# Differential attention in a two-block fp32 kernel: first branch weighed behind the bias pass, adaptive rows one by one, another order at the heads' ends and in the merge

## The chip, the cores and the metric

One core of a Trainium2 chip runs the whole program. The metric is the device time of one execution in microseconds (us); the figure given for a kernel is the median of its runs.

## The reference, cut to what matters

Two transformer blocks over 1024 tokens of width 1024, all in fp32. The change lies in the first block's mixer, whose three branches are merged under sigmoid gates:

```
h = rmsnorm(x); z = h @ w_in; gates = sigmoid(h @ w_gate + b_gate)     # 3 x 1024 gate columns
y_a = gmlp_mixer(...)                 # 256 wide
y_b = pool_mixer(...)                 # 256 wide
y_c = diff_attn_mixer(...)            # 4 heads, two softmaxes each: a = p0 - lam * p1, out = a @ v, rmsnorm
merged = g_a * (y_a @ proj_a) + g_b * (y_b @ proj_b) + g_c * (y_c @ proj_c)
x = x + merged @ w_out
```

The second block needs `ada_params(silu(c), w_ada, b_ada)` and the same for a context vector: products of a vector of 1024 with matrices of 1024 x 3072, which depend on nothing of the first block. The kernel computes them early, beside the first block's attention.

## The kernel before, in words

Every engine has a program of its own, written out by hand, and they meet only at semaphores. There is no scheduler: what stands first in an engine's program runs first.

**Dense units.** A unit is 1024 x 128 weights (512 KB). SyncE (SP) loads it, GpSimd (POOL) splits it into a high and a low part (lines 505 and 507), TensorE (PE) multiplies with three passes, 24 matmuls of 512 columns for each half of the tokens (line 530). The split of a unit begins when PE opens the unit before it. Results go to the PSUM halves 0 and 1. A half may be overwritten when its reader has counted `dn_out[half]`; `dense_order()` writes the order of the units down, and `dense` waits for the turn before it in the same half.

**The attention phase ("diff").** Four heads, each with eight tiles `t` of 128 queries; tile `t` has (t+1)*128 keys. In a tile the engines do:

- PE (`diff_head` of the tensor block): `turn_weights` transposes the weights of tile t (line 691; it waits for `aa_ready` and for PSUM pair 1, that is for the copy of the last product), a dense block in slot 0, `weigh_values` (line 700), the scores of tile t+2 (line 666), a dense block in slot 1.
- VectorE (DVE): `biased(h, t+1)` adds the bias to the scores and takes the row maxima (line 1740, twice), negates them (line 1744, 128x2); `combine(h, t+1)` follows ScalarE's exponentials (lines 1753 to 1756) and counts `aa_ready`; then the copy of the product (line 1800), then in slot 0 and slot 1 what the dense blocks need of VectorE.
- ScalarE (ACT): the copy of the transposed weights (line 1245), `exps(h, t+1)` (line 1228), the tanh of the gate blocks (line 1163).

**What fills the slots.** `head_slots()` deals out the blocks of each index i: gates `ga`, `gb`, `gc` (24 matmuls a half, read by ScalarE), and `pa`, `pb`, the projections of the first and the second branch (one unit together, 6 matmuls a half, so 12 in a slot). VectorE weighs `pa` and `pb` with their gates (`weighted`, line 1765) and adds them (line 1770). So `pb` in slot 1 needs `pa` weighed, and the next tile's gate block needs `pb` weighed. In this text a tile with `pa` in one slot and `pb` in the other is a pair tile; there are two of them in each head (tiles 2 and 6, in the last head 3 and 6).

**The adaptive rows.** 48 tiles of 128x1024 (`AW`, two buffers), loaded by SP with `load_ada`, reduced by `ada` on VectorE against the vector CL, and where k % 6 < 2 against CC too (line 1783: one pass or two). They run in pairs, one pair in each of the first 24 tiles, behind the copy of the product. The load of row k waits until row k-2 is done; it stands in SP's queue behind the tile's weight loads.

**Heads' ends and starts.** Behind tile 7 VectorE makes the norm's diagonal (line 1604), waits for PE's spread (line 571), and scales and splits the head's output (lines 1813, 1818). `head_start` then makes the values and the first scores, transposes the values (line 683), and ScalarE copies them to VC (line 1236) and frees the PSUM pair (line 1238), before the first `turn_weights`.

**The merge.** For each i of eight, VectorE takes `pc` of half 0 and half 1 times its gate (line 1859), adds it to M (line 1865), and then makes the low part of the M before (`merged_low`, line 1870), which waits for ScalarE's high part.

The slots, the places of the rows and the merge's loop are set by these lines of the kernel before:

```
        for place in [(t, 1) for t in range(2)][:len(free) - len(blocks)]:
            free.remove(place)
        for i in range(KC):
            merge(i)
            if i:
                merged_low(i - 1)
```

Of the kernel before, what the change touches and what calls it, by code (L numbers as in the profile page):

```python
# [27 lines left out]
P = 128  # L28
# [84 lines left out]
ADA_STEP = 2  # L113
# [3 lines left out]
def head_slots():  # L117
# [9 lines left out]
    for h in range(HEADS_C):  # L127
# [9 lines left out]
        for place in [(t, 1) for t in range(2)][:len(free) - len(blocks)]:  # L137
            free.remove(place)
# [5 lines left out]
SLOTS = head_slots()  # L144

# [43 lines left out]
def build(nc, t_in, out):  # L189
# [219 lines left out]
    def _(sp):  # L409
# [44 lines left out]
        step = 0  # L454
        for h in range(HEADS_C):
            for t in range(QT_N):
# [3 lines left out]
                if step == 0:  # L460
# [50 lines left out]
    def _(pe):  # L511
# [159 lines left out]
        def head_start(h):  # L671
# [32 lines left out]
        def diff_head(h):  # L704
            for t in range(QT_N):
                turn_weights(h, t)
                slot(h, t, 0)
# [5 lines left out]
                slot(h, t, 1)  # L713
# [368 lines left out]
    def _(act):  # L1082
# [91 lines left out]
        for j in range(2):  # L1174
            xts[0] += 1
            act.wait_ge(xt, xts[0])
            act.activation(YA[:, j * T:(j + 1) * T], TMP[j], ACT.Copy).then_inc(hi, 1)

# [61 lines left out]
        def diff_head(h):  # L1240
            last = h == HEADS_C - 1
            for t in range(QT_N):
                n = (t + 1) * P
                act.wait_ge(done[1], before("diff", 1) + 17 * h + 2 + 2 * t)
# [7 lines left out]
                slot(h, t, 0)  # L1252
# [30 lines left out]
        for half in range(2):  # L1283
            gate_out("ga", 0, half)
# [262 lines left out]
    def _(v):  # L1547
# [229 lines left out]
        def ada(k):  # L1777
# [14 lines left out]

        def diff_head(h):
            for t in range(QT_N):
                if t + 1 < QT_N:
                    v.wait_ge(done[1], before("diff", 1) + 17 * h + 2 + 2 * t)
                    biased(h, t + 1)
                    combine(h, t + 1)
# [4 lines left out]
                slot(h, t, 0)  # L1803
                step = h * QT_N + t
# [625 lines left out]
```

## Time and profile before

| | |
|---|---|
| median of 3 runs | 2733.97 us (2733.26 to 2734.22) |
| profiled execution | 2733.36 us, its span 2731.5 us |
| busy: PE, VectorE, ScalarE, GpSimd | 2564.0, 1375.3, 696.0, 660.6 us |
| granted TensorE clock, mean of the span | 0.978 |
| bytes moved | 158.16 MB, mean 58 GB/s |

The span is the profiled execution from its first to its last instruction; the time is the whole of that execution. PE is busy for nearly all of the span, so what counts is the time in which PE stands still, and the stretches in which its clock is granted at half (0.50, which is 1.2 GHz, where 1.00 is 2.4 GHz). The attention phase and the merge lie between 137 and 800 us of the span. A timeline row gives start, duration, engine, line, operation and count, and in brackets how long the engine had been idle before it and for whom.

### The profile page before, as it was taken

Reading aid. Unit: us, or ns where it says so; the run is one execution under the profiler, and the core shown is the slowest. Engines: PE = TensorE matmul, PEld = TensorE weight load, DVE = VectorE, ACT = ScalarE, POOL = GpSimd, SP = SyncE. Lnnn points to the kernel's source line nnn. Section 1 sums busy time; section 2 is a strip of 40 time slices with the busy share of each in tenths; the row PEclk is TensorE's granted clock in tenths of the full one; section 3 lists DMA queues with packets and bytes.
Section 4 is the critical chain, followed back from the end, with each engine's and each line's share of the span. In section 5 each row is a group of like instructions: output and inputs, shape, how many; then the busy total and the mean of one; then the engine's idle time right before and its main releaser. Section 6 shows DMA issues by size and latency. Waiting matters only on the chain.

```text
span 2731.5 us, 32633 instructions
## 1 busy us (share of the span) xinstructions
PE 2564.0 (94%) x12342; PEld 2106.0 (77%) x12342; DVE 1375.3 (50%) x1730; ACT 696.0 (25%) x973; POOL 660.6 (24%) x368
## 2 busy tenths in 40 slices
PE   7989998999899999999999989989999998899997
PEld 4867777777778788888888867878888887688876
DVE  5646363644364453145315564256676664533344
ACT  3222222222212111000000132145556652222121
POOL 1322222222233233333333332200000002222221
PEclk9999999999999999999999999999999999999998
DMA  4134242421322111111121111100000001110111
GB/s 154 47 101 139 85 124 93 131 93 47 133 68 85 46 46 46 54 46 46 48 67 46 54 56 33 45 24 9 8 15 8 8 9 56 31 39 31 38 39 69
DMA packets 44734, 158.16 MB, mean 58 GB/s; under 512 B 5453, under 2 KB 6733, under 8 KB 44527
## 3 DMA queue, kind: packets, MB, share of 16 engines
q1 hardware_dynamic: 38172, 132.94, 15.7%
q10 hardware_dynamic: 6482, 24.12, 2.4%
q8 instruction: 55, 0.90, 0.1%
q14 instruction: 25, 0.20, 0.0%
HBM read 143.67 MB, written 13.37 MB: 57 GB/s over the span
## 4 chain that ended last, share of the span: by engine, by line
PE 85%; DVE 9%; issue 3%; ACT 2%; DVEq 0%; ACTq 0%
PE PS L530 65%; PE PS L965 4%; PE PS L905 3%; PE PS L937 2%; PE PS L913 2%; PE PS L666 1%; PE PS L571 1%; PE PS L700 1%; PE PS L563 1%; DVE H L1626 1%; DVE SC L1783 1%; PE PS L691 1%; DVE PT L2118 1%; PE PS L1047 1%; PE PS L1062 0%
## 5 line engine op out<-in xcount | busy, mean ns | idle before, releaser
L530 PE MATMUL PS<-H,w_hl 128*128 128x512 f32 x6624 | 1548.9, 394 | 41.8 <-DVE H L1626 16.7
L530 PEld LDWEIGHTS PS<-H,w_hl 128*128 128x128 f32 x6624 | 1245.3, 189 | 327.8 <-issue 43.2
L505 POOL CAST w_hl<-w_raw 128x1024 fp32r<-128x1024 f32 x180 | 199.0, 1106 | 1997.2 <-PE PS L530 1587.0
L507 POOL TENSOR_TENSOR w_hl<-w_raw,w_hl 128x1024 fp32r<-128x1024 f32 x180 | 452.5, 2514 | 14.4
L530 PE MATMUL PS<-FF,w_hl 128*128 128x512 f32 x1056 | 239.8, 389 | 0.0
L530 PEld LDWEIGHTS PS<-FF,w_hl 128*128 128x128 f32 x1056 | 198.3, 188 | 41.1
L905 PE MATMUL PS<-CKV,QN 128*128 128x512 f32 (+1 forms) x576 | 146.9, 369 | 4.4 <-DVE QN L2082 4.4
L1360 ACT ACTIVATE SC<-SC,vec 128x1024 f32<-128x1024 f32 x22 | 25.4, 1153 | 392.5 <-DVE SC L1975 392.4
L965 PE MATMUL PS<-PT,CKT 128*128 128x256 f32 x960 | 121.4, 284 | 4.1 <-DVE PT L2118 4.1
L965 PEld LDWEIGHTS PS<-PT,CKT 128*128 128x128 f32 x960 | 117.7, 191 | 8.0 <-DVE PT L2118 7.3
L2118 DVE TENSOR_TENSOR PT<-PS,PT 128x512 fp32r<-128x512 f32 (+1 forms) x192 | 103.6, 595 | 30.6 <-ACT PT L1454 30.0
L905 PEld LDWEIGHTS PS<-CKV,QN 128*128 128x128 f32 x576 | 101.5, 193 | 22.2 <-issue 4.8
L2102 DVE TENSOR_REDUCE cols<-PS 128x1 f32<-128x1280 f32 x64 | 95.3, 1489 | 39.2 <-PE PS L913 39.2
L1454 ACT ACTIVATE PT<-PS 128x512 fp32r<-128x512 f32 (+1 forms) x192 | 87.0, 524 | 93.0 <-PE PS L937 92.9
L1894 DVE TENSOR_TENSOR X<-PS,X 128x1024 f32 (+2 forms) x25 | 29.5, 1182 | 157.3 <-PE PS L530 156.7
L937 PE MATMUL PS<-ident,E 128*128 128x128 f32 x640 | 84.5, 279 | 21.9 <-DVE G L2135 17.0
L913 PE MATMUL PS<-KPE,QPS 128*128 128x512 f32 (+1 forms) x384 | 103.1, 356 | 0.0
L1441 ACT ACTIVATE E<-PS,cols 128x1280 f32<-128x1280 f32 x64 | 85.4, 1334 | 53.9 <-DVE cols L2103 53.9
L937 PEld LDWEIGHTS PS<-ident,E 128*128 128x128 f32 x640 | 71.4, 142 | 28.3 <-DVE G L2135 13.0
L1970 DVE TENSOR_TENSOR SC<-PS,SC 128x1024 f32<-128x1024 f32 x22 | 27.0, 1226 | 129.5 <-PE PS L530 120.1
L530 PE MATMUL PS<-YB,w_hl 128*128 128x512 f32 x96 | 39.2, 586 | 40.7 <-DVE GTA L1765 40.7
L1905 DVE TENSOR_TENSOR SC<-SC 128x1024 f32<-128x1024 f32 (+1 forms) x36 | 62.0, 1721 | 30.4 <-ACT SC L1329 29.6
(289 smaller groups left out, 2409.2 us busy)
## 6 DMA issues: line engine op xcount, KB each, us to landing
w_raw<-in_units SPq DMA_DIRECT2D x182, 512.0 KB, 3.6
AW<-in_ada SPq DMA_DIRECT2D x48, 512.0 KB, 3.9
X<-in_x SPq DMA_DIRECT2D x8, 512.0 KB, 6.6
SC<-in_x ACTq DMA_DIRECT2D x8, 512.0 KB, 3.6
out<-X ACTq DMA_DIRECT2D x8, 512.0 KB, 3.1
m_part<-GTA ACTq DMA_DIRECT2D x7, 512.0 KB, 5.0
M<-m_part SPq DMA_DIRECT2D x7, 512.0 KB, 7.7
g_part<-GTB ACTq DMA_DIRECT2D x6, 512.0 KB, 3.4
```

What stands on the lines that cost most here:

```text
L505: pool.tensor_copy(hi_part, raw).then_inc(w_hi, 1)
L507: pool.tensor_tensor(lo_part, raw, hi_part.bitcast(F32), ALU.subtract).then_inc(w_split, 1)
L530: mm = pe.matmul(PS[:, out_at + a:out_at + a + m], w(s, wp, w0 + k), src[:, o:o + m], start=(k == 0 and wp == 0 and xp == 0), stop=(k == k ...
L905: mm = pe.matmul(PS[:, base + a:base + a + m], QN[:, qp_ * T + t * P:qp_ * T + (t + 1) * P], CKV[:, kp_ * TK + a:kp_ * TK + a + m], start= ...
L913: mm = pe.matmul(PS[:, base + a:base + a + m], QPS[:, t * P:(t + 1) * P], KPE[:, kp_ * TK + a:kp_ * TK + a + m], start=False, stop=(kp_ == 1))
L937: mm = pe.transpose(PS[:, bank + (kb - k0) * P:bank + (kb - k0 + 1) * P], E[:, (t % 2) * TK + kb * P:(t % 2) * TK + (kb + 1) * P], ident[: ...
L965: mm = pe.matmul(PS[:, 3584:3584 + GQ], CKT[:, vp * TK + kb * P:vp * TK + (kb + 1) * P], PT[:, xp * PTW + kb * GQ:xp * PTW + (kb + 1) * GQ ...
L1441: act.activation(E[:, (t % 2) * TK:(t % 2) * TK + TK], PS[:, base:base + TK], ACT.Exp, bias=cols[:, 16 + t % 2:17 + t % 2], scale=MLA_SCAL ...
L1454: act.activation(block_cols(0, t, k0, k1), bank_cols(bank, k0, k1), ACT.Copy).then_inc(pt_hi, 1)
L1905: v.tensor_tensor(total[:, part], total[:, part], sq[:, part], ALU.add).then_inc(sq_added, 1)
L2102: chain(v.tensor_reduce(cols[:, 22 + t % 2:23 + t % 2], PS[:, base:base + TK], AX, ALU.max))
L2118: v.tensor_tensor(block_cols(1, t, k0, k1), bank_cols(bank, k0, k1), block_cols(0, t, k0, k1).bitcast(F32), ALU.subtract).then_inc(pt_lo, 1)
```

## The change

Six edits; the arithmetic stays the same, and so does the count of every engine's instructions in the phase.

1. `head_slots()`: the empty slots lie elsewhere. In head 0 they were slot 1 of tiles 0 and 1 and are now slot 1 of tiles 5 and 7; in head 3 they were slot 1 of tiles 0 and 1 and are now slot 1 of tiles 4 and 5. So head 0's first pair tile is now tile 1; its second pair is split, `pa` in slot 0 of tile 5 and `pb` in slot 0 of tile 6. Head 3's first pair tile is now tile 2.
2. VectorE's slot 0 (the weighing of `pa`) moves from behind the copy of the product to right behind `biased`, ahead of `combine`.
3. The adaptive rows run one by one: one behind `biased` ("bias") and one behind the copy ("out") in each tile from head 0's tile 2 on, two more while VectorE waits for the norm's spread ("norm", written to ACC and not SQ), one behind the next head's first `combine` ("start"). SP's loads follow the same table.
4. Start of a head on PE: the value transposes go in two halves around the second scores; slot 0 of tile 0 runs ahead of `turn_weights`, on ScalarE too.
5. ScalarE before head 0: the tanh of `ga` 0 goes in between the two high parts of YA, and no longer behind the low parts; the load of the first bias goes ahead of both.
6. Merge on VectorE: the low part of M[i-1] goes between the two halves of `pc` i, ahead of the wait for half 1.

```diff
-        for place in [(t, 1) for t in range(2)][:len(free) - len(blocks)]:
+        for place in [(5, 1), (4, 1) if last else (7, 1)][:len(free) - len(blocks)]:
...
+def ada_places():
+    places = {}
+    n = 0
+    for h in range(HEADS_C - 1):
+        here = [("bias", t) for t in range(QT_N - 1)] + [("out", t) for t in range(QT_N)]
+        here = sorted((t, place) for place, t in here) + [(QT_N, "norm")] * 2 + [(QT_N, "start")]
+        for t, place in here:
+            if h == 0 and t < 2 or h == HEADS_C - 2 and place == "start" or n == ADA_TILES:
+                continue
+            places.setdefault((h, t, place), []).append(n)
+            n += 1
...
             dense("v", h, 1)
-            scores(h, 1)
+            take(1, b("diff", 1) + 17 * h)
             for half in range(2):
+                if half:
+                    scores(h, 1)
                 pe.wait_ge(dn_out[half], dn_turn["v", h] + 1)
-            take(1, b("diff", 1) + 17 * h)
-            for kb in range(QT_N):
...
         def diff_head(h):                                      # tensor
             for t in range(QT_N):
+                if t == 0:
+                    slot(h, t, 0)
                 turn_weights(h, t)
-                slot(h, t, 0)
+                slot(h, t, 1 if t == 0 else 0)
...
         load_bias(0)                                           # scalar
+        for j in range(2):
+            xts[0] += 1
+            act.wait_ge(xt, xts[0])
+            act.activation(YA[:, j * T:(j + 1) * T], TMP[j], ACT.Copy).then_inc(hi, 1)
+            gate_out("ga", 0, j)
...
                     biased(h, t + 1)                           # vector
+                    slot(h, t, 0)
+                    ada_at(h, t, "bias")
                     combine(h, t + 1)
...
-                slot(h, t, 0)
-                step = h * QT_N + t
-                if step < ADA_TILES // ADA_STEP:
...
-                    for k in range(step * ADA_STEP, (step + 1) * ADA_STEP):
-                        ada(k)
+                ada_at(h, t, "out")
+                if t + 1 == QT_N:
+                    slot(h, t, 0)
                 slot(h, t, 1)
...
+            norm_scale(h + before("diff", "norm"), h * 9 + (before("diff", 2) + 8), None, T, P, 1e-5)
+            ada_at(h, QT_N, "norm")
+            v.wait_ge(done[3], h * 9 + (before("diff", 3) + 9))
...
             combine(h, 0)
+            ada_at(h - 1, QT_N, "start")
...
+                if half == 0 and i:                            # merge
+                    merged_low(i - 1)
```

What the table puts where on VectorE is seen in head 1's tile 2 (a pair tile; ISA on AW is an adaptive pass, GTA<-GTA,PS the weighing of `pa`). Before:

```order
L1744 TENSOR_SCALAR cols<-cols 128x2
L1753 RECIPROCAL cols<-cols 128x2
L1754 TENSOR_TENSOR cols<-cols 128x1
L1755 TENSOR_SCALAR SC<-SC,cols 128x512
L1756 SCALAR_TENSOR_TENSOR SA<-SA,cols,SC 128x512
L1800 COPY SC<-PS 128x128
L1765 SCALAR_TENSOR_TENSOR GTA<-GTA,PS 128x512 x2
L1783 ISA SC,adac<-AW_107,CL 128x1024
L1783 ISA SC,adac<-AW_108,CL 128x1024
L1765 SCALAR_TENSOR_TENSOR GTB<-GTB,PS 128x512 x2
```

The same tile now (every line number is some twenty to thirty higher):

```order
L1789 SCALAR_TENSOR_TENSOR GTA<-GTA,PS 128x512 x2
L1807 ISA SC,adac<-AW_107,CL 128x1024
L1807 ISA SC,adac<-AW_107,CC 128x1024
L1777 RECIPROCAL cols<-cols 128x2
L1778 TENSOR_TENSOR cols<-cols 128x1
L1779 TENSOR_SCALAR SC<-SC,cols 128x512
L1780 SCALAR_TENSOR_TENSOR SA<-SA,cols,SC 128x512
L1832 COPY SC<-PS 128x128
L1807 ISA SC,adac<-AW_108,CL 128x1024
L1807 ISA SC,adac<-AW_108,CC 128x1024
L1789 SCALAR_TENSOR_TENSOR GTB<-GTB,PS 128x512 x2
```

The weighing of `pa` and an adaptive row stand ahead of the combining, and the two rows that now fall in this tile take two passes each, four in all where there were two.

On PE the start of head 1 was (SC is the values, SA the weights):

```order
L666 MATMUL PS<-KT,QT 128x256 x2
L683 MATMUL PS<-ident,SC 128x128 x8
L691 MATMUL PS<-ident,SA 128x128
L530 MATMUL PS<-H,w_hl 128x512 x24
L700 MATMUL PS<-AT,VC 128x128
L666 MATMUL PS<-KT,QT 128x384 x2
L530 MATMUL PS<-H,w_hl 128x512 x24
```

and is now:

```order
L703 MATMUL PS<-ident,SC 128x128 x4
L685 MATMUL PS<-KT,QT 128x256 x2
L703 MATMUL PS<-ident,SC 128x128 x4
L549 MATMUL PS<-H,w_hl 128x512 x24
L711 MATMUL PS<-ident,SA 128x128
L549 MATMUL PS<-H,w_hl 128x512 x24
L720 MATMUL PS<-AT,VC 128x128
L685 MATMUL PS<-KT,QT 128x384 x2
```

A dense block stands between the value transposes and the first transpose of weights; the second dense block of tile 0 moved ahead of `weigh_values`.

## Rows read from the trace of the kernel before

**Rows 1.** The page: the chain that ended last, by engine.
```profile
PE 85%; DVE 9%; issue 3%; ACT 2%; DVEq 0%; ACTq 0%
```

**Rows 2.** Who waited for whom, 137 to 912 us: total us, times, longest us.
```profile
PE PS L530 <- DVE GTA L1765: 40.7, 8, 6.5
...
PE PS L530 <- DVE GC L1859: 5.3, 5, 1.3
PE PS L691 <- ACTq L1238: 5.0, 4, 1.3
...
PE PS L530 <- DVE GTB L1765: 2.0, 2, 1.6
```

**Rows 3.** Stretches: start:end, length, PE busy (count), granted clock, DMA share, GB/s.
```profile
137.00:912.00 775.00, 710.60 (x3320) 0.97 0.31 98
154.40:157.80 3.40, 3.04 (x7) 0.50 0.47 183
```

**Rows 4.** Timeline of PE alone, 137 to 800 us.
```profile
154.75 7.17 PE L530 MATMUL PS<-H,w_hl 128*128 128x512 f32 x24 [2.48 <-ACT GTA L1163]
...
187.24 2.53 PE L666 MATMUL PS<-KT,QT 64*128 64x512 f32 x4 [2.96 <-DVEq L1743]
191.86 0.88 PE L691 MATMUL PS<-ident,SA 128*128 128x128 f32 x3 [2.09 <-DVEq L1801]
202.69 4.37 PE L530 MATMUL PS<-YB,w_hl 128*128 128x512 f32 x12 [3.98 <-DVE GTA L1765]
...
415.21 5.49 PE L530 MATMUL PS<-YB,w_hl 128*128 128x512 f32 x12 [6.05 <-DVE GTA L1765]
```

**Rows 5.** Timeline of head 1's tile 2, a pair tile.
```profile
347.08 3.01 PE L530 MATMUL PS<-YA,w_hl 128*128 128x512 f32 x12
...
349.39 1.88 DVE L1744 TENSOR_SCALAR cols<-cols 128x2 f32<-128x2 f32 x1
...
350.69 1.36 PE L666 MATMUL PS<-KT,QT 64*128 64x512 f32 x8
...
352.93 0.17 DVE L1753 RECIPROCAL cols<-cols 128x2 f32<-128x2 f32 x1 [1.66 <-ACT SC L1228]
...
353.84 0.75 DVE L1756 SCALAR_TENSOR_TENSOR SA<-SA,cols,SC 128x512 f32<-128x512 f32 x1
354.74 0.29 DVE L1800 COPY SC<-PS 128x128 f32<-128x128 f32 x1
355.27 1.28 DVE L1765 SCALAR_TENSOR_TENSOR GTA<-GTA,PS 128x512 f32<-128x512 f32 x2 [0.25 <-DVE SC L1800]
...
360.70 5.74 PE L530 MATMUL PS<-H,w_hl 128*128 128x512 f32 x24
```

**Rows 6.** Timeline: the first adaptive pass of all, and one in head 2.
```profile
181.05 1.22 DVE L1783 CUSTOM_DVE_ANT_0 SC<-AW,CL 128x1024 f32<-128x1024 f32 x1 [3.59 <-ACT CC L1257]
...
509.34 1.22 DVE L1783 CUSTOM_DVE_ANT_0 SC<-AW,CL 128x1024 f32<-128x1024 f32 x1
```

**Rows 7.** Timeline of head 1's tile 6, the second pair tile.
```profile
404.62 2.99 PE L530 MATMUL PS<-YA,w_hl 128*128 128x512 f32 x12
...
407.99 0.82 DVE L1744 TENSOR_SCALAR cols<-cols 128x2 f32<-128x2 f32 x1
...
411.32 0.17 DVE L1753 RECIPROCAL cols<-cols 128x2 f32<-128x2 f32 x1 [2.51 <-ACT SC L1228]
...
413.94 0.29 DVE L1800 COPY SC<-PS 128x128 f32<-128x128 f32 x1
...
421.37 1.87 PE L530 MATMUL PS<-H,w_hl 128*128 128x512 f32 x7
```

**Rows 8.** Timeline: VectorE at head 0's end, behind the norm's diagonal.
```profile
306.90 1.28 DVE L1813 SCALAR_TENSOR_TENSOR SC<-SC,cols,PS 128x1024 f32<-128x1024 f32 x1 [7.87 <-PE PS L571]
```

**Rows 9.** Timeline: two low parts in the merge.
```profile
760.59 3.41 DVE L1870 SCALAR_TENSOR_TENSOR H<-M,H 128x1024 fp32r<-128x1024 f32 x1
...
766.56 1.22 DVE L1870 SCALAR_TENSOR_TENSOR H<-M,H 128x1024 fp32r<-128x1024 f32 x1
```

More of the change, by code:

```diff
@@ L459, in _ @@
                         load_until(dn_unit[kind, i] + 2)
-                if step == 0:
+                if (h, t) == (0, 1):
                     sp.wait_ge(lo, before("diff", "split"))
-                if step < ADA_TILES // ADA_STEP:
-                    for k in range(step * ADA_STEP, (step + 1) * ADA_STEP):
+                for place in ("bias", "out"):
+                    for k in ADA_AT.get((h, t, place), []):
                         load_ada(k)
-                step += 1
             if h + 1 < HEADS_C:
                 load_until(dn_unit["v", h + 1] + 1)
+                for place in ("norm", "start"):
+                    for k in ADA_AT.get((h, QT_N, place), []):
+                        load_ada(k)
         load_until(dn_unit["gc", KC - 1] + 1)
@@ L677, in head_start @@
             dense("v", h, 1)
-            scores(h, 1)
+            take(1, b("diff", 1) + 17 * h)
             for half in range(2):
+                if half:
+                    scores(h, 1)
                 pe.wait_ge(dn_out[half], dn_turn["v", h] + 1)
-            take(1, b("diff", 1) + 17 * h)
-            for kb in range(QT_N):
-                mm = pe.transpose(PS[:, 1024 + kb * P:1024 + (kb + 1) * P], TMP0[:, kb * P:(kb + 1) * P],
-                                  ident[:, :])
+                for kb in range(4 * half, 4 * half + 4):
+                    mm = pe.transpose(PS[:, 1024 + kb * P:1024 + (kb + 1) * P], TMP0[:, kb * P:(kb + 1) * P],
+                                      ident[:, :])
             mm.then_inc(done[1], 1)
@@ L712, in diff_head @@
                     scores(h, t + 2)
-                slot(h, t, 1)
+                if t:
+                    slot(h, t, 1)
             if h == HEADS_C - 1:
@@ L1172, in _ @@
                 queries_keys(0, kind, half)
[L1174 to L1177, printed above, removed]
         def gate_out(kind, i, half):
@@ L1782, in ada @@
                 col = 2 * tile + n if tile < 2 else tile + 2
-                chain(v.tensor_tensor_reduce(out=SQ, in0=AW[k % 2][:, :], in1=row[:, :], scale=1.0,
+                chain(v.tensor_tensor_reduce(out=junk, in0=AW[k % 2][:, :], in1=row[:, :], scale=1.0,
                                              scalar=0.0, op0=ALU.mult, op1=ALU.add, accum_out=adac[:, col:col + 1]))
@@ L1791, in ada, with ada_at @@
                 chain(v.tensor_copy(modl[:, 2 * o:2 * o + 4], adac[:, 4:8]))
+        def ada_at(h, t, place):
+            for k in ADA_AT.get((h, t, place), []):
+                if k == 0:
+                    v.wait_ge(c_silu, 2)
+                ada(k, ACC if place == "norm" else SQ)
         def diff_head(h):
@@ L1797, in diff_head @@
                     biased(h, t + 1)
+                    slot(h, t, 0)
+                    ada_at(h, t, "bias")
                     combine(h, t + 1)
@@ L1802, in diff_head @@
                 v.sem_inc(oc_ready, 1)
-                slot(h, t, 0)
-                step = h * QT_N + t
-                if step < ADA_TILES // ADA_STEP:
-                    if step == 0:
-                        v.wait_ge(c_silu, 2)
-                    for k in range(step * ADA_STEP, (step + 1) * ADA_STEP):
-                        ada(k)
+                ada_at(h, t, "out")
+                if t + 1 == QT_N:
+                    slot(h, t, 0)
                 slot(h, t, 1)
-            norm_scale(h + before("diff", "norm"), h * 9 + (before("diff", 2) + 8), h * 9 + (before("diff", 3) + 8),
-                       T, P, 1e-5)
+            norm_scale(h + before("diff", "norm"), h * 9 + (before("diff", 2) + 8), None, T, P, 1e-5)
+            ada_at(h, QT_N, "norm")
+            v.wait_ge(done[3], h * 9 + (before("diff", 3) + 9))
             v.scalar_tensor_tensor(out=TMP0, in0=OC, scalar=cols[:, 6:7], in1=PS[:, 3072:4096],
```

13 lines of the change are left out of this document (6 added, 7 removed).

## Prediction

> **What bounds the kernel now.** I read the chain that ended last first: 85% of it is PE [rows 1]. So only PE's idle time and its half-clock stretches can be won. Next the waits of the attention phase and the merge [rows 2]: eight times PE stands before a `pb` block until VectorE has weighed `pa`, 40.7 us in all; four times 1.25 us at a head's start, for ScalarE's copy of the values; five times up to 1.3 us in the merge; twice, 2.0 us, for `pb`'s own weighing. The PE timeline adds 2.48 us before head 0, and 2.96 and 2.09 us in its second tile [rows 4]. These make some 60 us.
>
> The clock comes on top. Behind the idle 2.48 us, 24 matmuls took 7.17 us; the same block takes 5.74 us elsewhere [rows 4, 5], and the clock granted in that stretch was 0.50, the 1.2 GHz level [rows 3]. Behind 3.98 us idle twelve matmuls took 4.37 us, behind 6.05 us they took 5.49, where twelve at full clock take 3.01 [rows 4, 5]. Over 137 to 912 us the mean clock is 0.97 [rows 3], about 23 us of full-speed work. Gaps of 1.3 us show no such slowing. Waiting and clock together: some 80 us at most are there to be won.
>
> **Edit 5** lets the tanh of `ga` half 0 run when its matmuls are done, and no longer behind YA's low parts. The 2.48 us and the 7.17 - 5.74 = 1.4 us behind them go: **3.9**. Its two DMAs of c rows leave a little later and the bias load earlier; neither has a reader that waits on them now.
>
> **Edit 4** puts a 5.5 us dense block over the 1.0 us value copy: the four waits of 1.25 us go, **5.0**. Its cost would be on the path from the first turn to the second: bias pass and negation 2, exponentials 1.3, combining 1.3, copy 0.5, so some 5.3 us, against PE work of 7 (24 matmuls, weighing, scores, transpose). It fits; without that block it would wait at once.
>
> **Head 0, tiles 1 to 3.** VectorE waited 3.59 us for ScalarE's silu in order to start its first four adaptive passes [rows 6], and the scores and the next turn waited behind them: 2.96 and 2.09, then 3.98 at `pb` [rows 4]. At half clock the 2.53 and 0.88 lose half, 1.7, `pb` 4.37 - 3.01 = 1.4, and `pa` about as much. That is 13.5. Now the first row is due in tile 2, and the pair falls in tile 1, where rows are short and no adaptive pass stands. What stays: `pa` weighed 0.7 late behind the negation, and 0.3 because ScalarE's silu (3.4 us) delays one copy: 1.0. **12.5** won.
>
> **The pair tiles.** Here I lay VectorE's program down anew, in rows' durations. Take head 1's tile 2 [rows 5]. `pa` opens at 347.08. The negation ends at 351.27: it is 128x2 and takes 1.88 us, since it waits for GpSimd's split. PE is ready for `pb` at 350.69 + 1.36 = 352.05, and got it at 355.27 + 0.7. Now:
> - `pa` weighed 351.3 to 352.6 (1.28 for both halves); `pb` starts at 352.1, its wait is gone.
> - The adaptive row has two passes of 1.27 [rows 6]: to 355.2. Exponentials were ready at 352.9, so the combining (352.93 to 354.6, 1.67) now begins 2.3 late and ends at 357.0; the copy ends at 357.4 and the next turn begins at 357.6. `pb` was done at 354.85: PE idle 2.7.
> - The turn takes 0.4; then two passes more to 360.2, `pb` half 0 weighed at 361.0, the gate block at 361.1: PE idle 3.1.
>
> From `pa` to the gate block it was 360.70 - 347.08 = 13.6; the work in it is 8.35 (4.97 to PE's readiness; 2.73 for `pb`, half of a 24-matmul block's 5.46, which is its 5.74 without the last one's tail; 0.65 for the turn), so 5.3 were lost. Now 14.0, and the two gaps should bring the clock down for the block behind, by the rows above 1.4 to 2.5; I take 1.9. So this tile comes out 2.2 **worse**. Head 2's tile 2 has two-pass rows before as well (a further 1.6 for `GTB` [rows 2] and 0.4 of clock): 0.3 worse. Together **-2.5**.
>
> Tile 6 of heads 1 and 2 has one-pass rows. From [rows 7]: negation ends 408.8, `pa` weighed to 410.1, row to 411.5 (exponentials ready at 411.3, so it is hidden), combining to 414.1, copy to 414.5, turn at 414.7, second row to 416.0, `pb` half 0 weighed 416.7, gate block at 416.8. That is 12.2 us behind `pa` where it was 16.75; the work is 8.35, so 8.4 lost becomes 3.9, plus 0 to 1.4 of clock, 0.7 taken: **7.5** for the two.
>
> Head 0's second pair: `pa` in tile 5 with a two-pass row behind it and an empty slot 1. The turn of tile 6 comes 4.9 (negation) + 1.4 + 2.6 + 2.4 + 0.4 = 11.7 us after tile 5's, PE's cover is 0.85 + 2.73 + 1.3 + 2.3 = 7.2: 4.5 idle, 2.2 of clock, 0.5 in tile 6; 7.2 against 8.9 before (like [rows 7], with 0.5 for its four passes): **1.7**.
>
> Head 3 has no adaptive rows. First pair 5.4 to 0.45, second (turn 7 waits 2.1, `pb` 0.5, clock 0.7) 8.8 to 3.3; tile 4, now with one gate block of 5.5 us and a path of 9.9 against 9.2, costs 0.7: **9.7**.
>
> **The other rows.** Behind the norm's diagonal VectorE stood 7.87 us [rows 8]; two rows are at most three passes and three small copies there, 4.6. "Start" falls into about 5 idle us. In the ordinary tiles a row ahead of the combining makes the path about 10 us (negation 4.9, two passes 2.6, combining 1.7, copy 0.5), under PE's 13.7. SP's load of a row still waits for the row two before, more than one tile earlier; weights stay two units ahead. All nothing, while these covers hold; an adaptive row beyond the cover costs 1.27 a pass.
>
> **The merge.** Every second low part ran into GpSimd's split, 3.41 us instead of 1.22 [rows 9], and half 0 of the next `pc` stood behind it. Now it comes before half 1, which PE needs 2.7 us later. Three of the five waits [rows 2] go, **3.8**; the first and the last have other causes. A low part that starts inside a split is still held to its end, as the 3.41 was, and half 1 behind it; if that reached PE, the 3.8 would stay lost and the sum be 37.8. By the rule of the Trainium skill (SBUF — State Buffer, section "Who interferes with whom") a VectorE instruction with two SBUF inputs is blocked by a GpSimd instruction that reads SBUF, whatever its place in the program; by it the low parts of every second i are still held. Row and rule agree on the holding; whether it reaches PE is open.
>
> **Sum:** 3.9 + 5.0 + 12.5 - 2.5 + 7.5 + 1.7 + 9.7 + 3.8 = 41.6. Against the profiled 2733.36 (0.6 under the median) that gives 2692.
>
> **Rivals.**
> - *The clock stays up* behind the new, shorter gaps. For it: 1.3 us gaps leave it alone. Against: 2.48 us did not. The estimates 1.9 x 2, 0.7 x 3 and 2.2 go: 2684. The Trainium skill's page TensorE: Matmul & The Clock Gate, "Why this matters for your kernels", counts only longer idle gaps as costly; the 2.48 us row speaks against it.
> - *The rows eat the pairs.* If in tile 6 too the path is longer than laid down (a split or a late row ahead of the combining, both gaps at half clock), tile 6 of heads 1 and 2 and head 0's second pair win nothing: 9.2 less, 2701. For it: tile 2 shows how one more pass goes straight to PE.
> - *Slower than before.* The row ahead of `combine` sits on the path to the next turn in every tile. It decides once the path exceeds 13.7 us, 3.8 more than laid down, as when each row landed late behind a weight load in SP's queue. At 2.0 us past that in 23 tiles, 46 lost: 2738. Against: rows have over a tile to land.
> - *The merge wait survives*, by the holding above: the held part ends at most 1.2 us behind the point at which half 1 is due, and PE asks for it 2.7 us behind that, so I give it little. 2733.4 - 37.8 = 2696.
>
> **How the numbers follow.** Forecast as laid down, 2687 to 2697: 0.47. Merge wait survives, 2696: 0.08. Clock stays up, 2682 to 2687: 0.17. Rows eat the pairs, 2697 to 2707: 0.22. Slower: 0.03; something that leaves no gain: 0.03. The range 2682 to 2706 keeps out less than 2 in 10. A measurement of this kernel tells 0.2%, 5.5 us, from no change: faster 0.95, same 0.02, slower 0.03.
>
> **What would show it.** Right: no PE wait on the `pa` weighing over 1 us; no wait for the value copy; in tile 2 of heads 1 and 2 PE idle before the turn (2.7) and before the gate block (3.1), with clock 0.50 behind; a wait near 4.5 in head 0's tile 5 to 6; no merge wait but the first and last. Wrong: waits on `aa_ready` in ordinary tiles, or VectorE waiting for `AW` to land.

## The result and the profile after

The changed kernel takes **2694.67 us** (median of 4 runs, 2690.77 to 2699.11) against 2733.61 (2733.03 to 2734.22) for the kernel before, timed beside it: ratio 0.986, 95% interval 0.984 to 0.988. The prediction said 2692, and 2682 to 2706. The profiled execution has a span of 2692.9 us, 38.6 less than before. Run once more (x7, below) it gave 2694.95 (2691.10 to 2698.59). The changed kernel's own runs spread over 8 us, those of the kernel before over 1.

The page's chain by engine answers to [rows 1]; PE is still what bounds the kernel:

```profile
PE 86%; DVE 9%; issue 3%; ACT 2%; DVEq 0%; DMA 0%; ACTq 0%; SPq 0%
```

Where the time went is seen when the span is cut where the attention phase and the merge end, at the first matmul of the next projection. That matmul starts at 911.96 us before and at 871.36 now: the phase is 40.6 us shorter. Stretches of the changed kernel (start:end, length, PE busy, PE weight load, VectorE, ScalarE, GpSimd, granted clock, DMA share, GB/s):

```profile
137.00:871.00 734.00, 700.25 (x3321) 558.86 (x3319) 384.78 (x608) 176.10 (x289) 205.17 (x112) 0.98 0.33 104
871.00:2692.90 1821.90, 1735.98 (x8574) 1452.06 (x8574) 906.55 (x1017) 479.54 (x643) 419.65 (x234) 0.98 0.12 38
```

The second stretch was 1819.5 us before and holds none of the six edits: 2.1 us were given back there. The records of the granted clock show 78 us at 0.50 in it, and 67 us in the kernel before; the same kernel's other profile (x7, below) shows 71 us and 1819.6. So this part differs from one execution to the next, and the 40.6 us of the phase are what has to be explained. In the phase 24 us are at 0.50, where there were 51.

Who waited for whom, PE alone, 137 to 875 us (total, times, longest), against [rows 2]. One wait of 2.6 us, at the start of the next projection and the same before, is left out:

```profile
PE PS L711 <- DVEq L1833: 18.6, 8, 4.8
PE PS L549 <- DVE GTB L1789: 8.4, 6, 2.9
...
PE PS L549 <- DVE GC L1889: 1.5, 2, 1.3
PE PS L549 <- DVE GTA L1789: 1.4, 3, 0.5
```

The wait for the weighing of `pa` was 40.7 us in eight places and is 1.4 in three (line 1789 is the weighing; `GTA` is `pa`, `GTB` is `pb`). The wait for the value copy at a head's start is gone from the list, and that for `pc` in the merge fell from 5.3 to 1.5. In their place stand turns of weights that wait for VectorE (line 1833 follows the copy of a product; the combining is just ahead of it), 18.6 us, and gate blocks that wait for `pb`'s weighing, 8.4. The places, on PE's timeline (L711 transposes the weights, L549 is a dense matmul):

```profile
240.34 1.13 PE L711 MATMUL PS<-ident,SA 128*128 128x128 f32 x7 [4.78 <-DVEq L1833]
255.97 1.07 PE L711 MATMUL PS<-ident,SA 128*128 128x128 f32 x8 [3.05 <-DVEq L1833]
338.51 0.63 PE L711 MATMUL PS<-ident,SA 128*128 128x128 f32 x4 [2.40 <-DVEq L1833]
342.06 7.90 PE L549 MATMUL PS<-H,w_hl 128*128 128x512 f32 x24 [2.93 <-DVE GTB L1789]
...
398.08 1.06 PE L711 MATMUL PS<-ident,SA 128*128 128x128 f32 x8 [1.93 <-DVEq L1833]
400.37 5.69 PE L549 MATMUL PS<-H,w_hl 128*128 128x512 f32 x24 [1.22 <-DVE GTB L1789]
...
547.73 1.52 PE L711 MATMUL PS<-ident,SA 128*128 128x128 f32 x8 [1.93 <-DVEq L1833]
550.01 8.05 PE L549 MATMUL PS<-H,w_hl 128*128 128x512 f32 x24 [0.77 <-DVE GTB L1789]
...
681.22 1.07 PE L711 MATMUL PS<-ident,SA 128*128 128x128 f32 x8 [1.72 <-DVEq L1833]
```

240 and 256 us are the turns behind head 0's tiles 5 and 6 (its first pair, in tile 1, leaves a wait of 0.35), 338 and 342 head 1's tile 2 (head 2's reads alike: 2.35 and 2.93, then 24 matmuls in 8.46), 398 and 400 tile 6 of head 1, 548 and 550 that of head 2, 681 that of head 3. A block of 24 matmuls takes 5.7 us at full clock; 7.90, 8.05 and 8.46 are blocks partly at half clock.

### The profile page after: what moved, and what is told of

It is laid out like the page before. It is cut to its first block, busy times and chain, and to the rows that moved or that the text cites. A ratio compares the mean times of both kernels' runs of the same rounds, so it can differ in the third digit from the quotient of the medians.

```text
span 2692.9 us, 32636 instructions
## 1 busy us (share of the span) xinstructions
PE 2554.2 (95%) x12342; PEld 2098.5 (78%) x12342; DVE 1373.7 (51%) x1730; ACT 695.8 (26%) x973; POOL 660.0 (25%) x368
## 4 chain that ended last, share of the span: by engine, by line
PE 86%; DVE 9%; issue 3%; ACT 2%; DVEq 0%; DMA 0%; ACTq 0%; SPq 0%
PE PS L549 66%; PE PS L988 4%; PE PS L928 3%; PE PS L960 2%; PE PS L936 2%; PE PS L685 1%; PE PS L590 1%; PE PS L582 1%; DVE SC L1807 1%; DVE H L1650 1%; PE PS L720 1%; DVE PT L2148 1%; DVE cols L2132 1%; PE PS L1070 1%; PE PS L1085 1%
## 5 line engine op out<-in xcount | busy, mean ns | idle before, releaser
L549 PE MATMUL PS<-H,w_hl 128*128 128x512 f32 x6624 | 1554.8, 395 | 46.4 <-DVE H L1650 17.5
L549 PEld LDWEIGHTS PS<-H,w_hl 128*128 128x128 f32 x6624 | 1250.1, 190 | 333.6 <-issue 46.6
L526 POOL TENSOR_TENSOR w_hl<-w_raw,w_hl 128x1024 fp32r<-128x1024 f32 x180 | 453.2, 2518 | 14.4
L549 PE MATMUL PS<-FF,w_hl 128*128 128x512 f32 x1056 | 239.8, 389 | 0.0
L549 PEld LDWEIGHTS PS<-FF,w_hl 128*128 128x128 f32 x1056 | 198.2, 188 | 41.2
L960 PEld LDWEIGHTS PS<-ident,E 128*128 128x128 f32 x640 | 70.3, 140 | 29.7 <-DVE G L2165 13.1
L1353 ACT ACTIVATE SC<-X 128x1024 f32 (+2 forms) x27 | 26.1, 966 | 199.4 <-DVE X L1926 152.5
L936 PEld LDWEIGHTS PS<-KPE,QPS 128*128 128x128 f32 x384 | 68.8, 191 | 11.1
```

Of the source, the lines that this page charges most:

```text
L526: pool.tensor_tensor(lo_part, raw, hi_part.bitcast(F32), ALU.subtract).then_inc(w_split, 1)
L549: mm = pe.matmul(PS[:, out_at + a:out_at + a + m], w(s, wp, w0 + k), src[:, o:o + m], start=(k == 0 and wp == 0 and xp == 0), stop=(k == k ...
L936: mm = pe.matmul(PS[:, base + a:base + a + m], QPS[:, t * P:(t + 1) * P], KPE[:, kp_ * TK + a:kp_ * TK + a + m], start=False, stop=(kp_ == 1))
L960: mm = pe.transpose(PS[:, bank + (kb - k0) * P:bank + (kb - k0 + 1) * P], E[:, (t % 2) * TK + kb * P:(t % 2) * TK + (kb + 1) * P], ident[: ...
```

## The experiments

Nine runs followed, eight of other kernels and one of the changed kernel again, each timed in three or five rounds beside the kernel before, whose median was 2732.5 (x1 to x4), 2732.9 (x5 to x7) and 2733.9 (x8, x9). Differences from the changed kernel are taken from its first median, 2694.67. The kernel before moved by 1.3 us between these sessions and the changed kernel's own runs spread over 8 us, so a difference of one or two us means nothing.

### x1: edit 2 undone

```diff
                     biased(h, t + 1)
-                    slot(h, t, 0)
                     ada_at(h, t, "bias")
...
-                ada_at(h, t, "out")
-                if t + 1 == QT_N:
-                    slot(h, t, 0)
+                slot(h, t, 0)
+                ada_at(h, t, "out")
                 slot(h, t, 1)
```

> The changed kernel with edit 2 alone undone: the weighing of pa stands behind the copy of the product again, rows and all else stay. My theory (the weighing's place is the largest single part): PE waits before pb for 4 to 6 us in tile 1 of head 0, tiles 2 and 6 of heads 1 to 3, and the later waits before the turn and the gate block shrink. By the rows of before, worked out place by place: head 1 and 2 tile 2 about 0, tile 6 of heads 1 and 2 +4 each, head 3 +5 each, head 0 +9; together 28 us over the changed kernel (2694.7), 2723. Rival (the adaptive rows' places carry the gain): within 8 us of 2695, since the new pb wait only takes the place of the wait before the next turn.

Measured: 2717.11 (2716.88 to 2717.36), 22.4 over the changed kernel. The waits of `pb` for `pa` are back in seven places, 3.77 to 6.11 us each, and the block behind each is at half clock for a part (twelve matmuls take 3.0 at full clock). One of them, on PE's timeline:

```profile
348.20 4.95 PE L549 MATMUL PS<-YB,w_hl 128*128 128x512 f32 x12 [5.00 <-DVE GTA L1789]
```

The waits list of this run gives them together as 36.0 us, and the records of the clock 58 us at 0.50 in the phase. So the rival falls and the place of the weighing is the largest single lever. It is worth less than the 36 us of waits, because with it in place other waits open in the same tiles. It is also less than the 28 of the theory. Head 2's tile 6 grows by only 1.5 where 4 was booked, since the changed kernel's profile already had 2.8 us of half clock there; the rest is not resolved.

### x2: edit 3 undone, the rows in pairs behind the copy

```diff
+    return {(k // 2 // QT_N, k // 2 % QT_N, "out"): [k // 2 * 2, k // 2 * 2 + 1] for k in range(ADA_TILES)}
...
-                if (h, t) == (0, 1):
+                if (h, t) == (0, 0):
```

> The changed kernel with edit 3 alone undone: the rows run in pairs behind the copy from head 0's tile 0 on, none at the norm or the start. My theory: head 0's first tiles wait for the silu and four passes again (+11), tile 2 of head 1 gets better (-3.5, its rows take one pass and none stands ahead of the combining), head 2's stays, tile 6 of heads 1 and 2 +2.5 each, head 0's tiles 5 and 6 -5 (no row ahead of the combining): 2702, 2697 to 2708. Rival (one row at a time is what makes the change work): 20 us or more over 2695, as PE waits for aa_ready or pb in most pair tiles.

Measured: 2707.78 (2706.33 to 2708.99), 13.1 over the changed kernel, more than the theory's middle. PE's timeline:

```profile
188.25 2.93 PE L674 MATMUL PS<-KT,QT 64*128 64x512 f32 x4 [6.23 <-DVEq L1756]
...
409.03 8.07 PE L538 MATMUL PS<-H,w_hl 128*128 128x512 f32 x24 [3.25 <-DVE GTB L1778]
...
502.57 7.44 PE L538 MATMUL PS<-H,w_hl 128*128 128x512 f32 x24 [5.62 <-DVE GTB L1778]
```

With the pair behind the copy, nothing stands ahead of the turn in tile 2 (its wait of 2.40 is gone), but all passes stand ahead of `pb`'s weighing: 3.08 and 5.62 before the gate block in tile 2 of heads 1 and 2, 3.25 in head 1's tile 6. The rival, 20 us or more, falls. The 6.23 is head 0's early tile: VectorE stands 3.59 us for ScalarE's silu (the same number as in [rows 6]), four passes follow, and the scores wait for the bias pass behind them. The scores themselves then take 2.93 where 1.13 is usual, so that one place costs 8.0 us, more than half of the 13.1.

### x3: edits 4, 5 and 6 undone

The head's start, the tanh of `ga` 0 and the merge's low part are in their old order; edits 1 to 3 stay.

```diff
-            take(1, b("diff", 1) + 17 * h)
             for half in range(2):
-                if half:
-                    scores(h, 1)
                 pe.wait_ge(dn_out[half], dn_turn["v", h] + 1)
+            take(1, b("diff", 1) + 17 * h)
...
-                if t == 0:
-                    slot(h, t, 0)
                 turn_weights(h, t)
-                slot(h, t, 1 if t == 0 else 0)
+                slot(h, t, 0)
...
-            gate_out("ga", 0, j)
...
-                if half == 0 and i:
-                    merged_low(i - 1)
+            if i:
+                merged_low(i - 1)
```

> The changed kernel with edits 4, 5 and 6 undone together (they lie at different places of the span, so the trace keeps them apart). My theory: PE waits again 2.5 us before head 0 with about 1.4 us of half clock behind, 1.25 us at four heads' starts, and 1.3 us three times in the merge: 3.9 + 5.0 + 3.8 = 12.7, so 2707.4. Rival (in the new surroundings these waits were covered anyway, or their removal only lengthens the next wait): under 6 us.

Measured: 2710.66 (2707.81 to 2713.07), 16.0 over the changed kernel. The phase is 16.3 longer in the profiles. PE's timeline:

```profile
154.75 7.28 PE L549 MATMUL PS<-H,w_hl 128*128 128x512 f32 x24 [2.48 <-ACT GTA L1182]
171.17 0.30 PE L710 MATMUL PS<-ident,SA 128*128 128x128 f32 x1 [1.25 <-ACTq L1252]
188.37 0.68 PE L719 MATMUL PS<-AT,VC 128*128 128x128 f32 x4 [1.58 <-ACTq L1261]
...
740.49 11.17 PE L549 MATMUL PS<-OCS,w_hl 128*128 128x512 f32 x48 [1.28 <-DVE GC L1883]
...
765.35 5.73 PE L549 MATMUL PS<-OCS,w_hl 128*128 128x512 f32 x24 [1.28 <-DVE GC L1883]
```

The rival falls, and the three terms come back as booked: 2.48 and 7.28 - 5.74 = 1.5 before head 0, 1.25 in each of four heads, three waits of 1.23 to 1.28 in the merge: 12.8. Of the 3.2 beyond that, 1.2 is the copy of head 0's tile 1 (1.58 where the changed kernel has 0.36: ScalarE does the silu at that time); the rest is not resolved, and the changed kernel's own spread is as large.

### x4: no adaptive row in the pair tiles

```diff
-            if h == 0 and t < 2 or h == HEADS_C - 2 and place == "start" or n == ADA_TILES:
-                continue
+            if h == 0 and t < 2 or (h, t) in busy:
+                continue
+            for place, rows in (("bias", 1 if t + 1 < QT_N else 0), ("out", 2)):
...
+ADA_AT = ada_places({(0, 5), (0, 6)} | {(h, t) for h in (1, 2) for t in (2, 6)})
```

> The changed kernel with another table of rows: none in tiles 2 and 6 of heads 1 and 2 and none in tiles 5 and 6 of head 0; the ordinary tiles take one row ahead of the combining and two behind the copy. My theory (two-pass rows on VectorE make the waits left in pair tiles, and the half clock follows them): tile 2 of heads 1 and 2 loses its gaps of 2.4 and 2.9 us and the slow block behind, 7.5 each; tile 6 keeps about 1.9 before the turn and loses the gap behind, 1.5 each and 2.3 of clock in one; head 0: 4.8 becomes 2.2, 3.05 becomes about 1, clock 1.5. Together -24: 2671. Rival (PE waits there for the combining's own length and for GpSimd's split, rows or none): less than 8 us better. Second rival (three rows an ordinary tile are too many, PE then waits for aa_ready there, or VectorE for the load of a row): slower than 2690.

Measured: 2675.90 (2674.89 to 2677.85), ratio 0.979 (0.978 to 0.981), 18.8 under the changed kernel. The tile-2 gaps of 2.4 and 2.93 with their 2 to 3 us of half clock are gone. PE's timeline:

```profile
238.44 1.73 PE L716 MATMUL PS<-ident,SA 128*128 128x128 f32 x7 [3.15 <-DVEq L1838]
252.01 1.07 PE L716 MATMUL PS<-ident,SA 128*128 128x128 f32 x8 [1.55 <-DVEq L1838]
330.08 3.06 PE L554 MATMUL PS<-YB,w_hl 128*128 128x512 f32 x12 [0.64 <-DVE GTA L1794]
334.07 5.73 PE L554 MATMUL PS<-H,w_hl 128*128 128x512 f32 x24 [0.24 <-DVE GTB L1794]
...
460.23 1.99 PE L690 MATMUL PS<-KT,QT 64*128 64x512 f32 x4 [1.64 <-DVEq L1772]
```

So the rows were the cost in tile 2: of 7.5 us, 0.64 + 0.24 are left. Both rivals fall. The gain is 5 us short of the theory's 24. Turn 7 keeps a wait of 1.75 without a row in its tile, head 0's two gaps stayed longer than expected (2.2 and about 1), and a new 1.64 came at 460, in an ordinary tile of head 2 with three rows, where a small copy took 2.24 us (see the last section).

### x5: head 0's second pair kept whole

```diff
-        for place in [(5, 1), (4, 1) if last else (7, 1)][:len(free) - len(blocks)]:
+        for place in ([(4, 1), (5, 1)] if last else [(2, 1), (3, 1)])[:len(free) - len(blocks)]:
...
+ADA_AT = ada_places({(h, t) for h in range(3) for t in ((2, 3, 6) if h == 0 else (2, 6))})
```

(Two "out" rows in the other tiles, one in a tile 0.)

> On top of x4: head 0's empty slots lie in tiles 2 and 3 and its second pair stays whole in tile 6; no rows in head 0's tiles 2, 3 and 6; one row and not two behind the copy in tile 0. My theory (the split pair over tiles 5 and 6 cannot cover VectorE's path, whatever stands in it): the 3.15 and 1.55 us waits there with 2 us of half clock become 0.5 and 1.75, as in the other heads' tile 6, tile 2 costs at most 0.7, and head 2's 1.64 at the scores goes: 4.5 us under x4, 2671.5. Rival (short tiles anywhere give the same wait): within 1.5 us of x4's 2675.9.

Measured: 2666.84 (2665.37 to 2672.29), 9.1 under x4, twice what was expected. Head 0's tile 6 now reads as in the other heads, and the profile has no record at half clock in the phase:

```profile
195.68 0.63 PE L716 MATMUL PS<-ident,SA 128*128 128x128 f32 x4 [1.48 <-DVEq L1838]
239.47 3.04 PE L554 MATMUL PS<-YB,w_hl 128*128 128x512 f32 x12 [0.50 <-DVE GTA L1794]
244.24 1.06 PE L716 MATMUL PS<-ident,SA 128*128 128x128 f32 x8 [1.74 <-DVEq L1838]
```

The gaps of 3.15 and 1.55 became 0.50 and 1.74, and head 0's tile 2 has a new 1.48 where at most 0.7 was expected. The 1.64 at 460 and 0.6 before `pb` in tile 2 of heads 1 and 2 are gone too. All of PE's waits for VectorE in the attention phase fall from 15.8 to 12.1 us, and 1.4 us of half clock go with them. The profiled phase is 6.3 us shorter than x4's, the rest of the span 2.6. Only the 6.3 can be the edit's, and it changed slots and rows together, so it does not part the two; x8 does.

### x6: the negation on ScalarE

VectorE hands the row maxima over and ScalarE negates them in front of its exponentials.

```diff
-            v.tensor_scalar(cols[:, 8 + o:10 + o], cols[:, 54:56], -1.0, None, ALU.mult).then_inc(neg_ready, 1)
-            v.wait_ge(neg_ready, h * 8 + (t + 1))
+            v.sem_inc(max_ready, 1)
...
-            act.wait_ge(neg_ready, h * 8 + (t + 1))
+            act.wait_ge(max_ready, h * 8 + (t + 1))
+            act.activation(cols[:, 8 + 2 * (t % 2):10 + 2 * (t % 2)], cols[:, 54:56], ACT.Copy,
+                           scale=-1.0).then_inc(neg_ready, 1)
+            act.wait_ge(neg_ready, h * 8 + (t + 1))
```

> x5 with the negation of the two maxima on ScalarE, in place of VectorE's 128x2 instruction that lasted up to 1.9 us beside GpSimd's split. My theory (the 128x2 instruction is held by the split and sets the path in the pair tiles): the weighing of pa begins 0.8 us sooner in tile 6 and 1.7 in tile 2; ScalarE's step costs 0.2 to 0.3; the wait before turn 7 falls from 1.75 to about 1.1 in four places, that before pb to nothing in seven: 4 to 5 us under x5. Rival (the whole of VectorE stands still while GpSimd's split runs, so the next instruction is held instead): no difference, or slower by the ScalarE step.

Measured: 2660.78 (2659.44 to 2661.65), ratio 0.973 (0.972 to 0.975): 6.1 under x5, the fastest kernel of this study, 33.9 us under the changed kernel and 72 under the kernel before. The 32 negations, on VectorE in the changed kernel and on ScalarE here (groups by line: busy us, mean ns):

```profile
L1768 DVE TENSOR_SCALAR cols<-cols 128x2 f32<-128x2 f32 x32 | 33.7, 1052 | 4.8
```
```profile
L1250 ACT ACTIVATE cols<-cols 128x2 f32<-128x2 f32 x32 | 6.5, 204 | 58.5 <-DVEq L1777 58.4
```

Two numbers for each partition took VectorE 1052 ns in the mean, and 170 ns where no split of GpSimd ran beside them. The waits before `pb` (0.4 to 0.5) are gone. The first of PE's waits in the phase:

```profile
PE PS L717 <- DVEq L1841: 7.3, 5, 1.8
```

All that is left of the turn waits is 1.6 to 1.8 us at turn 7 of each head; these stayed, where about 1.1 was expected, so the held negation was not their cause. The rival of a standstill of the whole engine, with no gain, falls.

### x7: the changed kernel again

> The changed kernel itself once more. On its half clock: my theory (a wait of 2 to 3 us can be followed by half clock or not, as it falls, and the longer ones nearly always are): the waits of PE come out as in the first profile within 0.1 us each, tile 2 of heads 1 and 2 has half clock behind it again, while tile 6 of heads 1 and 2 (1.9 and 0.8 to 1.2 us) may differ from the first profile; single executions differ by up to 8 us. Rival (the clock follows from the program alone): the same blocks are slow as in the first profile, and the executions agree within 2 us.

Measured: 2694.95 (2691.10 to 2698.59). All waits but three are within 0.1 of the first profile's: turn 7 of head 0 is 2.83 in place of 3.05, and the gate blocks in tile 6 of heads 1 and 2 wait 0.40 and 0.52 in place of 1.22 and 0.77. The clock is not so regular:

```profile
397.66 1.90 PE L711 MATMUL PS<-ident,SA 128*128 128x128 f32 x8 [1.91 <-DVEq L1833]
399.95 6.26 PE L549 MATMUL PS<-H,w_hl 128*128 128x512 f32 x24 [0.40 <-DVE GTB L1789]
```

In head 1's tile 6 these eight transposes took 1.90 and the block 6.26; in the first profile, behind the same 1.93 us, they took 1.06 and 5.69. The slower transposes arrive 0.84 later at the gate block and wait 0.82 less there, so that part of the half clock cost nothing. Both profiles have half clock in tile 2 of heads 1 and 2. So gaps of this size bring the clock down in one execution and not in another. Whether the changed kernel's 8 us between runs come from it is not shown: x6 and x5 both have no half clock in their profiled phase, and x6 spreads over 2.2, x5 over 6.9.

### x8: edit 1 undone, the empty slots where they were

```diff
-        for place in [(5, 1), (4, 1) if last else (7, 1)][:len(free) - len(blocks)]:
+        for place in [(t, 1) for t in range(2)][:len(free) - len(blocks)]:
```

> The changed kernel with edit 1 alone undone: the empty slots are again slot 1 of tiles 0 and 1 of heads 0 and 3. Everything else stays as changed. Theory (the prediction's, edit 4: the block in slot 0 of tile 0 now runs ahead of the first turn, so slot 1 must hold the cover of the second turn): with slot 1 of tile 0 empty nothing dense stands between the turns of tiles 0 and 1 in heads 0 and 3. VectorE's and ScalarE's path there is about 5.3 us, PE's own work 1.5: 3.8 us idle twice, and 1.9 of half clock behind each, 11.4. Head 0's pair falls in tile 2 with two two-pass rows and costs what tile 2 of head 1 costs in the changed kernel, 2.4 + 2.9 idle and 2.9 of clock, 8.2. Head 0's second pair is whole again in tile 6: about 2.7 idle and 1 of clock in place of 4.8 + 3.05 and 2, 6 less. 2694.7 + 11.4 + 8.2 - 6 = 2708 (2702 to 2714). Rival: edit 1 matters for head 0's pair tiles alone and the second turn is no later than before (covered by the work around it): 2697, and no wait of turn 1 over 1.3 us. If edit 1 gave what the prediction booked under head 0 by itself, 12.5 + 1.7 would go: 2709, but with the waits in tile 2 alone.

Measured: 2709.08 (2707.08 to 2709.23), 14.4 over the changed kernel. PE's timeline:

```profile
172.37 0.46 PE L720 MATMUL PS<-AT,VC 128*128 128x128 f32 x2 [1.03 <-ACTq L1267]
176.55 0.66 PE L711 MATMUL PS<-ident,SA 128*128 128x128 f32 x2 [2.81 <-DVEq L1833]
...
621.98 0.61 PE L711 MATMUL PS<-ident,SA 128*128 128x128 f32 x2 [2.44 <-DVEq L1833]
```
```profile
256.84 1.06 PE L711 MATMUL PS<-ident,SA 128*128 128x128 f32 x8 [1.93 <-DVEq L1833]
259.13 5.73 PE L549 MATMUL PS<-H,w_hl 128*128 128x512 f32 x24 [1.22 <-DVE GTB L1789]
```

The rival falls: where slot 1 of tile 0 is empty, PE stands 1.03 + 2.81 = 3.8 us around turn 1 in head 0, and 1.05 + 2.44 = 3.5 in head 3; the two transposes behind take 0.66 and 0.61 where they take 0.44 at full clock, and the dense blocks behind them 8.02 and 7.26 where 5.74 is the full rate. Head 0's pair in tile 2 reads as head 1's does, 2.40 and 2.93. Its second pair, now whole, costs 0.46 + 1.93 + 1.22 = 3.6 us in tile 6 with no half clock (the second fence), though the table of rows is the changed kernel's. In the kernel before, with these same slots and PE's old order, turn 1 of head 0 did not wait. So edit 4 takes the cover of that turn away, and edit 1 gives it back. What edit 4 would give or cost without edit 1 no run shows.

### x9: edit 2 alone, on the kernel before

```diff
                     biased(h, t + 1)
+                    slot(h, t, 0)
                     combine(h, t + 1)
...
-                slot(h, t, 0)
+                if t + 1 == QT_N:
+                    slot(h, t, 0)
                 step = h * QT_N + t
```

> The kernel before with edit 2 alone: VectorE weighs pa right behind the bias pass, everything else as before. It asks whether the edits' shares add up. Theory: they overlap. Undone from the changed kernel, edit 2 gave 22.4 us, edit 3 13.1, edits 4 to 6 together 16.0. With edit 2 alone the eight waits of PE for the weighing of pa (40.7 us) go, but the two adaptive rows behind the copy then stand before the weighing of pb, as in the run with rows in pairs: waits of 3 to 5.6 us before the gate blocks in tile 2 and 1.8 + 3 in tile 6. So it is the run with rows in pairs plus edits 4 to 6 undone: 2707.8 + 16.0 = 2724 (2718 to 2729), a gain of 10. Rival: the shares add up, edit 2 is worth its 22.4 by itself: 2733 - 22.4 = 2710 (2707 to 2714).

Measured: 2723.72 (2721.91 to 2724.85), 10.1 under the kernel before. PE's timeline:

```profile
154.75 5.72 PE L530 MATMUL PS<-H,w_hl 128*128 128x512 f32 x24 [2.48 <-ACT GTA L1163]
...
266.32 7.54 PE L530 MATMUL PS<-H,w_hl 128*128 128x512 f32 x24 [5.18 <-DVE GTB L1765]
...
513.58 8.41 PE L530 MATMUL PS<-H,w_hl 128*128 128x512 f32 x24 [5.62 <-DVE GTB L1765]
```

Put on alone, edit 2 gives 10.1; taken away last, it costs 22.4. The rival, that the shares add up, falls. The 40.7 us of waits for `pa` go, and a good part comes back before the next gate block, since the pair of rows is now all that `pb`'s weighing waits behind. The shares of the edits do not add up: undone one at a time they are 14.4 (edit 1), 22.4 (2), 13.1 (3) and 16.0 (4 to 6), 65.9 in all, and together 38.9.

The first line is of another kind. Up to there x9 runs as the kernel before does, with the same gap of 2.48 us ahead of the same block at the same time; but the block took 5.72 here, at full clock, and 7.17 there. So 1.4 of the profiled gain is not edit 2's.

## Why the prediction was right

The forecast was 41.6 us in the phase, and the phase gave 40.6; 2.1 of them were lost again in the part that no edit touches. The total is closer than its terms: head 0's second pair came out 2.3 worse than booked and head 3 1.6 better, which largely cancel by luck, and where half clock falls differs between executions. Step by step:

- **Edit 5, 3.9.** Right. The 2.48 us gap is gone, and x3 brings it back with 1.5 of clock. The clock's 1.4 of the 3.9 hangs on the execution: in x9 the same gap had none behind it.
- **Edit 4, 5.0.** Right, with x3's four waits of 1.25. The sentence that it "would wait at once" without the block is borne out by x8, 3.8 us at turn 1.
- **Head 0, tiles 1 to 3, 12.5 with 1.0 left.** Right: 0.36 and 0.35 are left.
- **Tile 2 of heads 1 and 2, 2.5 worse.** Right in kind and size. Said: 2.7 before the turn, 3.1 before the gate block, 1.9 of clock. Found: 2.40, 2.93, and 7.90 - 5.74 = 2.2 or 8.46 - 5.74 = 2.7. Sum said 7.7, found 7.5 and 8.0. The order of VectorE's work as laid down is what ran:

```profile
330.41 1.92 DVE L1768 TENSOR_SCALAR cols<-cols 128x2 f32<-128x2 f32 x1
...
332.36 1.28 DVE L1789 SCALAR_TENSOR_TENSOR GTA<-GTA,PS 128x512 f32<-128x512 f32 x2
...
333.56 1.22 DVE L1807 CUSTOM_DVE_ANT_0 SC<-AW,CL 128x1024 f32<-128x1024 f32 x1
...
336.20 0.17 DVE L1777 RECIPROCAL cols<-cols 128x2 f32<-128x2 f32 x1
```

The reciprocal that opens the combining has no wait in front of it: the two passes delayed it, as said, and not ScalarE.
- **Tile 6 of heads 1 and 2, 7.5 better.** Right: 3.9 idle was said, 0.42 + 1.93 + 1.22 = 3.6 and 0.46 + 1.93 + 0.77 = 3.2 were found. Of the clock 0.7 was taken for each; it was 0 in head 1 and 2.8 in head 2.
- **Head 0's second pair, 1.7 better: the step that failed.** The wait before tile 6's turn was 4.78 (said 4.5), but "0.5 in tile 6" was 3.05 at the turn of tile 7. With 1.7 us of clock behind the first gap (1.13 and 4.52 where 0.93 and 3.01 are the full rate; 2.2 was said) the place cost 9.5 us where 7.2 was said. It had cost 8.9 before, so the change won nothing here; it lost about 0.6. Tile 6 was not laid down as the others were: between its bias pass and its combining stand the weighing of `pb`, the add and an adaptive pass. VectorE and GpSimd there:

```profile
247.76 1.23 DVE L1794 TENSOR_TENSOR GTA<-GTA,GTB 128x1024 f32<-128x1024 f32 x1
247.86 2.02 POOL L524 CAST w_hl<-w_raw 128x1024 fp32r<-128x1024 f32 x1 [14.33 <-PE PS L549]
248.90 2.06 DVE L1807 CUSTOM_DVE_ANT_0 SC<-AW,CL 128x1024 f32<-128x1024 f32 x1
249.97 3.24 POOL L526 TENSOR_TENSOR w_hl<-w_raw,w_hl 128x1024 fp32r<-128x1024 f32 x1
...
251.32 1.91 DVE L1778 TENSOR_TENSOR cols<-cols 128x1 f32<-128x1 f32 x1
```

The add and the pass run into GpSimd's cast and split, and a 128x1 product of the combining then stands out the split. The pass and the product take 0.8 + 1.75 us over their free durations of 1.2 and 0.16. Ahead of this the two passes of a row behind the late copy held the bias pass back to 243.25. Three runs part the causes. With the rows as they are and the pair whole (x8) the place costs 3.6 us. With the pair divided and no rows (x4) it costs 3.15 + 1.55 and 1.4 of clock, 6.1. With neither (x5) it costs 0.50 + 1.74 = 2.2. Both x8 and x5 pay for their empty slots elsewhere, in tile 0 and in tile 2. So both the rows and the divided pair were in it, and the divided pair was the larger.
- **Head 3, 9.7.** A little better than said: 0.24, 0.47, 0.48 and 1.72 are left, 2.9, where 4.5 was said. The 0.7 of clock did not come.
- **The merge, 3.8.** Right: 1.5 of 5.3 is left, at the first and the last. The rival that the wait survives falls, although its mechanism is there. Every second low part is still held, as the rule of the Trainium skill has it (SBUF — State Buffer, "Who interferes with whom": an instruction of VectorE with two SBUF inputs contends with a GpSimd instruction that reads SBUF). The changed kernel's GpSimd and VectorE:

```profile
723.73 3.26 POOL L526 TENSOR_TENSOR w_hl<-w_raw,w_hl 128x1024 fp32r<-128x1024 f32 x1
```
```profile
725.86 2.22 DVE L1902 SCALAR_TENSOR_TENSOR H<-M,H 128x1024 fp32r<-128x1024 f32 x1 [0.22 <-ACT H L1326]
```

It takes 2.22 where the free one takes 1.23, and half 1 of `pc` follows late. PE runs 168 matmuls of the merge without a gap, so it does not see it.

Of the other rivals: *the clock stays up* is wrong for tile 2, where both profiles show blocks of 7.9 to 8.5 us, and the page TensorE: Matmul & The Clock Gate of the Trainium skill ("Why this matters for your kernels"), which counts only longer gaps as costly, is not borne out by gaps of 2.4 and 2.9 us with only four transposes between them; full clock was kept in head 1's tile 6 once, and behind the 2.48 us of x9. *The rows eat the pairs* came true at head 0's second pair alone. The load of a row was late nowhere that PE saw.

## What to carry to other kernels

Before moving an instruction on a hand-written engine program, lay the whole tile down again, row by row, with the durations of the trace, the held ones among them; the place where that was skipped missed most. Moved work only helps where cover is left: taking the adaptive rows out of the tiles where PE waits twice for VectorE gave some 19 us, and in the ordinary tiles that took them one wait of 1.6 us came up. And measure edits both alone and taken away from the whole, since two edits on one wait give each other their value.

## What the runs showed of the hardware that was not expected

- **Tiny VectorE instructions are held too.** The 128x2 negation took 1.92 us beside a split of GpSimd, 0.17 without; a 128x1 product 1.91; in x4 a 128x4 copy 2.24, inside the split at 454.26 (2.40 long):

```profile
454.26 2.40 POOL L531 TENSOR_TENSOR w_hl<-w_raw,w_hl 128x1024 fp32r<-128x1024 f32 x1
454.44 2.24 DVE L1820 COPY modl<-adac 128x4 f32<-128x4 f32 x1
```

The adaptive pass right behind it (456.72, 1.22 us) was free. Moving the negation off the engine gained 6.1 us.
- **The holding goes both ways.** GpSimd's cast takes 1.04 us free and 2.02 beside VectorE's add, its split 2.37 to 2.41 free and 3.24 to 3.27 where an adaptive pass or the merge's add to M (line 1897) was still running as it opened.
- **The half clock is no fixed price.** It followed gaps of 2.4 and 2.9 us with four transposes (0.6 us) between them in both profiles of the changed kernel, gaps of 1.9 and 0.4 to 1.2 in some, and the gaps of 1.6 to 1.8 at turn 7 in x4 to x6 not once. Behind the single gap of 2.48 us it came in the kernel before and in x3 and not in x9. Which executions get it stays open.
